# A hybrid decoder trunk with expert retrieval: token rows held in PSUM for the expert dot products, and one pair of banks for the sums

## The chip, the cores and the metric

The kernel runs on one core of a Trainium2 chip. The metric is the device time of one execution in microseconds (us). The time before is 3547.99 us, the median of 3 runs (3546.83 to 3550.83).

## What is computed

Two layers over 512 tokens of width 1024, all in float32. Each layer first mixes three branches (causal pooling, a diagonal state space, dilated attention) through gates and an output projection. Then each token retrieves 128 experts (8 heads of 16) out of 16384. The second half is what the change touches:

```python
def eval_chunk(args):            # chunks of 128 tokens
    hx, e, g = args
    a = jnp.einsum('cd,ckd->ck', hx, u_tab[e])
    return jnp.einsum('ck,ckd->cd', g * jax.nn.gelu(a), v_tab[e])
```

`hx` are the normalized rows of 128 tokens, `e` their 128 expert numbers each, `u_tab` and `v_tab` two tables of 16384 rows of 1024 floats.

## The kernel before, in words

**Tiles and picks.** A tile is 128 tokens, one per partition. Four tiles in each of two layers make 8 tiles (`TILES`). A pick is one expert of every token of a tile, and a tile has 128 picks (`PICKS`), so there are 1024 picks in all. For each pick GpSimd (POOL) issues two gathers by an indirect DMA (line 906). One fetches 128 rows of the first table into one of 6 buffers `rows_u`, the other 128 rows of the second table into one of 6 buffers `rows_v`. Each brings 128 x 4 KB = 512 KB. POOL waits before a gather until its buffer is free: for `rows_u` until VectorE (DVE) has done the dot product six picks back, for `rows_v` until the sum six picks back is done.

**Dots.** For each pick DVE multiplies the 128 rows of `rows_u` with the 128 token rows in `h_tok` and adds up each product (`dot`, line 2105, one custom instruction of 128x1024, the product written over the row). Both inputs lie in SBUF; `h_tok` and `rows_u` are pieces of one tensor `heap`, so the trace shows the dot as heap<-heap. Groups of 8 picks then pass through the GELU on ScalarE (ACT, line 1450) and `weigh` (line 2116), which gives each pick its weight per token.

**Sums.** Twelve picks later the row of `rows_v`, times its weight, is added to the tile's sum. For most picks TensorE (PE) does it (`sum_pick`, line 1166): ACT makes a diagonal matrix of the weights (line 1430), and two matmuls 128x512 accumulate into a pair of PSUM banks. For some odd picks DVE does it (line 1803), into `tile_sum` in SBUF. Tiles take turns on two pairs of banks, 4 and 5 for even tiles, 6 and 7 for odd ones.

**Drain.** At a tile's end (`drain`) DVE joins the PSUM sum and `tile_sum` (lines 2082 and 2084), PE turns the result into columns (8 transposes, line 960), and DVE adds it to `xT` (line 2091). Because the next tile sums into the other pair, its first sum waits only for the drain of the tile two back.

**The token rows.** `h_tok` has two slots, by the tile's parity. PE transposes the normalized columns, and ACT copies them from PSUM to `h_tok` (line 1376, `htok`), after all dots of the tile that had the slot before.

**The order of work.** `make_plan` writes the program as a list of slots. Each slot has at most one dot (`u`) and one sum (`v`), and then a budget of other work for PE, ACT and DVE: the projections, attention, top-16 searches and so on of the next stage, which is computed while the experts of the earlier tiles are retrieved. Every engine runs its instructions in the order of the slots; `GATHERS` lists POOL's gathers in that order too. A stage is 256 tokens, so there are 4. Banks 0 to 3 of PSUM are the ring for all this other work; in the first stage, before the first sums, all 8 banks are. The weights come by other DMAs, issued from the SP queue, into 6 buffers `ring`.

## Time and profile before

| | before |
|---|---|
| median of 3 runs | 3547.99 us |
| profiled execution, its own time | 3563.16 us |
| span of the profiled execution | 3561.4 us |
| PE busy | 3145.3 us (88%) |
| DVE busy | 2528.4 us (71%) |
| POOL busy | 2364.8 us (66%) |
| ACT busy | 962.3 us (27%) |
| moved by DMA | 1305.56 MB, mean 367 GB/s |

The span is from the first to the last instruction of one profiled execution, and its own time is a little longer. Busy time counts the instructions alone. On POOL the issue of a gather counts, which is the time in which it makes the descriptors of the DMA, not the transfer itself. The profiled execution took 15 us more than the median.

### The profile page before, as it was taken

The page shows a single profiled execution, that of the slowest core. Times are in us where ns is not written, and L with a number is a line of the kernel's source. Part 1 is how long each engine was busy: PE and PEld are TensorE (multiplying, and loading weights), DVE is VectorE, ACT ScalarE, POOL GpSimd, SP SyncE. Part 2 cuts the span into 40 slices and gives each one's busy share as a digit, 9 for nine tenths or more (in the row PEclk, how much of TensorE's full clock was granted, in tenths as well). Part 3 has the DMA queues.
Part 4 walks back from the last instruction along what each step waited for, and adds up shares of the span by engine and source line. Part 5 has one row for each costly group of instructions (what it writes and reads, how often), then busy time and mean ns, then how long its engine had stood idle before and what let it go on. Part 6 is the DMA issues. An engine that isn't in the chain of part 4 may idle for free.

```text
span 3561.4 us, 37721 instructions
## 1 busy us (share of the span) xinstructions
PE 3145.3 (88%) x11468; PEld 2012.2 (57%) x11468; DVE 2528.4 (71%) x6159; ACT 962.3 (27%) x2092; POOL 2364.8 (66%) x2114
## 2 busy tenths in 40 slices
PE   8989999979997999968998999979997996667775
PEld 7778756646675656645675656645675652222222
DVE  6556598887656888877656898877666899545444
ACT  2332233343221233332221334333211232111111
POOL 1010276777767776677767777777767777777775
PEclk9989999989999999989999999989999999999998
DMA  5345699999999999999999999999999999999997
GB/s 174 107 175 178 235 407 400 383 397 395 385 409 409 405 392 403 388 400 407 396 409 409 409 405 396 382 397 394 392 409 409 406 390 373 368 373 397 407 408 286
DMA packets 363512, 1305.56 MB, mean 367 GB/s; under 512 B 40432, under 2 KB 44912, under 8 KB 363184
## 3 DMA queue, kind: packets, MB, share of 16 engines
q0 software_dynamic: 298960, 1087.79, 78.1%
q1 hardware_dynamic: 64352, 215.35, 15.9%
q8 instruction: 95, 1.56, 0.2%
q14 instruction: 105, 0.86, 0.1%
HBM read 1288.30 MB, written 14.68 MB: 366 GB/s over the span
## 4 chain that ended last, share of the span: by engine, by line
POOL 36%; PE 31%; issue 13%; DMA 12%; DVE 8%; ACT 0%; DVEq 0%; SPq 0%; POOLq 0%; ACTq 0%
POOL heap L906 36%; PE ps L948 14%; DMA heap<-table_v,heap 11%; PE ps L1166 11%; DVE heap L2105 2%; PE ps L1008 2%; DVE heap L1803 1%; PE ps L1103 1%; PE ps L1047 1%; PE ps L1087 0%; DMA ring<-ssm_par 0%; PE ps L1149 0%; PE ps L1053 0%; PE ps L1019 0%; PE ps L1065 0%
## 5 line engine op out<-in xcount | busy, mean ns | idle before, releaser
L1166 PE MATMUL ps<-heap 128*128 128x512 f32 x3224 | 1599.1, 623 | 345.1 <-DMA heap<-table_v,heap 285.2
L906 POOL DMA_INDIRECT heap<-table_u,heap x1024 | 1162.6, 1135 | 436.2 <-issue 293.7
L2105 DVE CUSTOM_DVE_ANT_0 heap<-heap 128x1024 f32<-128x1024 f32 x1024 | 1243.4, 1220 | 294.0 <-DMA heap<-table_u,heap 286.2
L906 POOL DMA_INDIRECT heap<-table_v,heap x1024 | 1167.6, 1140 | 410.6 <-issue 271.2
L1166 PEld LDWEIGHTS ps<-heap 128*128 128x128 f32 x3224 | 597.7, 196 | 1047.7 <-issue 782.7
L948 PE MATMUL ps<-hT,ring 128*128 128x256 f32 x3840 | 894.6, 383 | 11.2 <-DVE hT L1922 6.2
L948 PEld LDWEIGHTS ps<-hT,ring 128*128 128x128 f32 x3840 | 734.9, 192 | 224.7 <-issue 131.5
L1803 DVE SCALAR_TENSOR_TENSOR heap<-heap 128x1024 f32<-128x1024 f32 x211 | 271.0, 1284 | 362.9 <-issue 242.6
L1430 ACT ACTIVATE heap<-ident,heap 128x128 f32<-128x128 f32 x806 | 297.4, 394 | 543.2 <-PE ps L1166 310.8
L1450 ACT ACTIVATE heap<-heap 128x8 f32<-128x8 f32 x128 | 26.7, 208 | 497.0 <-DVE heap L2105 496.4
L1103 PE MATMUL ps<-temp,ring 128*128 128x256 f32 x640 | 150.6, 383 | 1.5 <-ACT temp L1316 1.0
L1103 PEld LDWEIGHTS ps<-temp,ring 128*128 128x128 f32 x640 | 121.9, 192 | 29.5 <-issue 13.9
L877 POOL DMA_DIRECT2D ssm_par<-heap x8 | 4.5, 566 | 185.4 <-DVEq L1665 185.4
L1335 ACT ACTIVATE temp<-ps 128x512 f32<-128x512 f32 x48 | 28.7, 597 | 350.9 <-PE ps L948 350.8
L948 PE MATMUL ps<-temp,ring 128*128 128x256 f32 x512 | 116.2, 385 | 0.0
L1450 ACT ACT_TABLE_LOAD x89 | 114.2, 1283 | 3.0
L948 PEld LDWEIGHTS ps<-temp,ring 128*128 128x128 f32 x512 | 99.1, 194 | 23.6 <-issue 10.6
L1269 ACT ACTIVATE temp<-ps 32x512 f32<-32x512 f32 x96 | 56.5, 588 | 160.0 <-PE ps L948 159.2
L1008 PE MATMUL ps<-ring,hT 128*128 128x256 f32 x384 | 89.3, 380 | 0.0
L1008 PEld LDWEIGHTS ps<-ring,hT 128*128 128x128 f32 x384 | 72.8, 190 | 25.4 <-issue 17.2
L2105 DVE DVE_READ_ACCUMULATOR2_ANT heap<- 128x1 f32 x1024 | 84.0, 82 | 0.0
L1349 ACT COPY temp<-ps 128x512 f32<-128x512 f32 x32 | 18.7, 586 | 220.9 <-PE ps L948 220.9
(256 smaller groups left out, 2615.2 us busy)
## 6 DMA issues: line engine op xcount, KB each, us to landing
ring<-weights SPq DMA_DIRECT2D x344, 512.0 KB, 7.4
ring<-ssm_par SPq DMA_DIRECT2D x48, 512.0 KB, 7.4
heap<-table_u,heap POOLq DMA_INDIRECT x1024, 9.0
heap<-table_v,heap POOLq DMA_INDIRECT x1024, 8.9
ssm_par<-heap POOLq DMA_DIRECT2D x20, 512.0 KB, 6.6
ring<-weights SPq DMA_DIRECT2D x20, 256.0 KB, 6.1
xT<-x_cm SPq DMA_DIRECT2D x2, 1024.0 KB, 9.3
ssm_par<-heap POOLq DMA_DIRECT2D x8, 256.0 KB, 4.0
```

Source lines behind the costliest of these rows:

```text
L906: pool.indirect_dma_start(rows[:, j, :], None, table, bass.IndirectOffsetOnAxis(expert[:, tile % 2, k:k + 1], 0)).then_inc(landed, 16)
L948: mm = pe.matmul(ps[:, b, i * width:(i + 1) * width], piece(u, name, k * P, P), src[:, k, :], start=(k == 0), stop=(k == rows_n - 1))
L1008: mm = pe.matmul(ps[:, b, tt * 256:(tt + 1) * 256], hT[:, k, tt * P:(tt + 1) * P], piece(u, names[k // 4], (k % 4) * 256, 256), start=(k = ...
L1047: end(pe.matmul(ps[:, b, 0:width], query, kT[part_, m, first:first + width], start=True, stop=True))
L1103: mm = pe.matmul(ps[:, b, j * N:(j + 1) * N], piece(u, ("branch", mm2, br), (rows_n * j + k) * P, P), src[:, k, :], start=(k == 0), stop=( ...
L1166: mm = pe.matmul(ps[:, 4 + 2 * (tile % 2) + half, :], diag[:, PE_TURN[v] % DIAGS, :], rows_v[:, v % NV, half * 512:(half + 1) * 512], star ...
L1269: ins = act.activation(turn_s[to, :], ps[at:at + 32, b, :], ACT.Copy, scale=1.0 if q % 2 else -1.0)
L1335: act.activation(sig[u][:, n % 2, :], ps[:, b, :], ACT.Sigmoid).then_inc(gate_sig, 1)
L1430: act.activation(diag[:, n % DIAGS, :], ident[:], ACT.Copy, scale=w_st[:, g % 3, v % GROUP:v % GROUP + 1]).then_inc(diag_ready, 1)
L1450: act.activation(gelu_st[:, n % 3, :], act_st[:, n % 3, :], ACT.Gelu_apprx_tanh).then_inc(gelued, 1)
L1803: dve.scalar_tensor_tensor(tile_sum, rows_v[:, v % NV, :], w, tile_sum, ALU.mult, ALU.add).then_inc(v_free[v % NV], 1)
L2105: dve.tensor_tensor_reduce(row, row, h_tok[:, tile % 2, :], 1.0, 0.0, ALU.mult, ALU.add, act_st[:, g % 3, pick % GROUP:pick % GROUP + 1]). ...
```

## The change

ACT gets a new piece of work, `hload`, once per tile: after the last dot of the tile before, it copies the tile's token rows from `h_tok` into PSUM banks 6 and 7 (two copies of 128x512). The dots take their second input from there. The sums of all tiles use the one pair 4 and 5, so that the first sum of a tile waits until the drain of the tile before is over (`x_home`). The plan keeps the dots back from a tile's first pick until `hload` is done, the sums until the drain is over, and dots at most 12 picks ahead of sums (`u - v <= LAG`).

```diff
-        htok = (("htok", u // PICKS // 2, u // PICKS % 2, 1), 1)
-        if u < TILES * PICKS and ready([chosen, htok], s):
+        if u < TILES * PICKS and ready([chosen, (("hload", u // PICKS), 0)], s) and u - v <= LAG:
             slot["u"] = u
-        if v < u and v // GROUP * GROUP + GROUP <= u and (v // GROUP * GROUP + GROUP - 1) in end_of \
+        if v < u and (v % PICKS or v == 0 or ready([(("drain", v // PICKS - 1), 2)], s)) and v // GROUP * GROUP + GROUP <= u and (v // GROUP * GROUP + GROUP - 1) in end_of \
...
+        htok = (("htok", tokens // 2, tokens % 2, 1), 1)
+        if tokens < TILES and u == tokens * PICKS and ready([htok], s) and (u == 0 or end_of[u - 1] < s):
+            queue["ACT"].appendleft([("hload", tokens), 0, 1, s])
+            tokens += 1
...
+SUM_BANK, TOKEN_BANK = 4, 6
...
-                        mm = pe.transpose(ps[:, 4 + 2 * (tile % 2) + c // 4, (c % 4) * P:(c % 4 + 1) * P],
+                        mm = pe.transpose(ps[:, SUM_BANK + c // 4, (c % 4) * P:(c % 4 + 1) * P],
...
-                if k == 0 and tile >= 2:
-                    pe.wait_ge(x_home, 2 * (tile - 1))
+                if k == 0 and tile:
+                    pe.wait_ge(x_home, 2 * tile)
...
-                    mm = pe.matmul(ps[:, 4 + 2 * (tile % 2) + half, :], diag[:, PE_TURN[v] % DIAGS, :],
+                    mm = pe.matmul(ps[:, SUM_BANK + half, :], diag[:, PE_TURN[v] % DIAGS, :],
...
-                        act.wait_ge(dotted, PICKS * (2 * u - 1 + t))
+                        act.wait_ge(h_there, 2 * (2 * u - 1 + t))
...
+                elif kind == "hload":
+                    tile = item[1]
+                    act.wait_ge(h_copied, 2 * (tile + 1))
+                    if tile:
+                        act.wait_ge(dotted, PICKS * tile)
+                    else:
+                        for b in range(TOKEN_BANK, TOKEN_BANK + 2):
+                            act.wait_ge(bank_free[b], BANK_TOTAL[b])
+                    for half in range(2):
+                        act.copy(ps[:, TOKEN_BANK + half, :], h_tok[:, tile % 2, 512 * half:512 * half + 512]).then_inc(h_there, 1)
+                        yield
...
                 if pick % PICKS == 0:
-                    dve.wait_ge(h_copied, 2 * (tile + 1))
+                    dve.wait_ge(h_there, 2 * (tile + 1))
...
-                dve.tensor_tensor_reduce(row, row, h_tok[:, tile % 2, :], 1.0, 0.0, ALU.mult, ALU.add,
+                token = ps[:, TOKEN_BANK:TOKEN_BANK + 2, :].rearrange("p i c -> p (i c)")
+                dve.tensor_tensor_reduce(row, row, token, 1.0, 0.0, ALU.mult, ALU.add,
```

The plan has 1249 slots before and 1270 in the changed kernel; the number of sums on DVE goes from 218 to 221. Where a tile ends, the order moves. On PE, around the end of the second tile, before (L1166 are the sums, L948 and L1116 projections and key scores of the next stage, L960 the transposes of the drain):

```order
L1166 MATMUL ps<-heap 128x512 x2
L948 MATMUL ps<-hT,ring 128x256 x4
L1166 MATMUL ps<-heap 128x512 x2
L960 MATMUL ps<-ident,heap 128x128 x8
L1166 MATMUL ps<-heap 128x512 x2
L948 MATMUL ps<-hT,ring 128x256 x3
L1166 MATMUL ps<-heap 128x512 x4
```

and in the changed kernel, whose line numbers are higher (L1173 the sums, L955 and L1123 the other work, L967 the transposes):

```order
L955 MATMUL ps<-hT,ring 128x256 x3
L1173 MATMUL ps<-heap 128x512 x4
L1123 MATMUL ps<-keysT,temp 128x128 x4
L955 MATMUL ps<-hT,ring 128x256 x9
L967 MATMUL ps<-ident,heap 128x128 x8
L955 MATMUL ps<-hT,ring 128x256 x7
L1173 MATMUL ps<-heap 128x512 x4
```

Before, sums of the next tile stand ahead of the transposes; now all sums of the next tile stand behind them, and 16 projection matmuls stand between the last sum of one tile and the first of the next. On DVE at the same place, before (L2105 are the two instructions of a dot, L2082 and L2091 the two ends of the drain, the rest is the search for the 16 best):

```order
L2105 ISA heap<-heap 128x1024
L2105 ISA heap 128x1
L2082 TENSOR_TENSOR heap<-heap,ps 128x512 x2
L1845 MAX_INDEX heap<-heap 128x8
L2105 ISA heap<-heap 128x1024
L2105 ISA heap 128x1
L1850 MAX heap<-heap 128x8 x2
L1854 MAX_INDEX heap<-heap 128x8 x2
L1856 TENSOR_TENSOR heap<-heap 128x256
L2105 ISA heap<-heap 128x1024
L2105 ISA heap 128x1
L2091 TENSOR_TENSOR xT<-xT,ps 128x4x128 x2
```

and changed (L2123 the dot, L2099 and L2108 the drain):

```order
L2123 ISA heap<-heap,ps 128x1024
L2123 ISA heap 128x1
L2099 TENSOR_TENSOR heap<-heap,ps 128x512 x2
L1922 TENSOR_SCALAR heap<-heap 128x16
L1924 SCALAR_TENSOR_TENSOR heap<-heap 128x16
L2123 ISA heap<-heap,ps 128x1024
L2123 ISA heap 128x1
L1930 TENSOR_SCALAR heap<-heap 128x16
L1856 MAX heap<-heap 128x8 x2
L1860 MATCH_REPLACE heap<-heap 128x128 x2
L2108 TENSOR_TENSOR xT<-xT,ps 128x4x128 x2
```

One dot instead of two stands between the two ends of the drain, and the dots read `ps` beside `heap`. On ACT the new copies stand between its usual work (L1448 the diagonals, L1369 and L1371 copies of key scores, L1468 the GELU):

```order
L1468 ACT_TABLE_LOAD
L1468 ACTIVATE heap<-heap 128x8
L1448 ACTIVATE heap<-ident,heap 128x128
L1396 COPY ps<-heap 128x512 x2
L1369 COPY heap<-ps 128x256
L1371 COPY heap<-ps 128x256
L1448 ACTIVATE heap<-ident,heap 128x128
```

Whatever stands behind the two copies on ACT, a diagonal for the sums among it, waits with them for the last dot of the tile.

## Rows read from the trace of the kernel before

**Rows 1.** The page: span, busy time of each engine, DMA rate in 40 slices.

```profile
span 3561.4 us, 37721 instructions
PE 3145.3 (88%) x11468; PEld 2012.2 (57%) x11468; DVE 2528.4 (71%) x6159; ACT 962.3 (27%) x2092; POOL 2364.8 (66%) x2114
GB/s 174 107 175 178 235 407 400 383 397 395 385 409 409 405 392 403 388 400 407 396 409 409 409 405 396 382 397 394 392 409 409 406 390 373 368 373 397 407 408 286
```

**Rows 2.** One line's instructions: gathers, duration min/median/max, idle before them, time to landing.

```profile
L906 POOL DMA_INDIRECT heap<-table_u,heap x1024: 935/942/2025, 412.0 to 3515.4; - x171
L906 POOL DMA_INDIRECT heap<-table_v,heap x1024: 935/941/2819, 435.5 to 3537.1; - x171
...
  issue: 564.9, 1830
...
DMA to landing us min/median/max: 4.4/8.9/19.6
```

**Rows 3.** Costliest groups of the page: busy, mean ns of one, idle before.

```profile
L906 POOL DMA_INDIRECT heap<-table_u,heap x1024 | 1162.6, 1135 | 436.2 <-issue 293.7
L2105 DVE CUSTOM_DVE_ANT_0 heap<-heap 128x1024 f32<-128x1024 f32 x1024 | 1243.4, 1220 | 294.0 <-DMA heap<-table_u,heap 286.2
L906 POOL DMA_INDIRECT heap<-table_v,heap x1024 | 1167.6, 1140 | 410.6 <-issue 271.2
L1803 DVE SCALAR_TENSOR_TENSOR heap<-heap 128x1024 f32<-128x1024 f32 x211 | 271.0, 1284 | 362.9 <-issue 242.6
```

**Rows 4.** Stretches: length; PE, PEld, DVE, ACT, POOL busy (count); PE clock; DMA share; GB/s.

```profile
600.00:700.00 100.00, 100.00 (x350) 61.70 (x349) 85.54 (x250) 32.76 (x71) 70.26 (x62) 1.00 1.00 383
1400.00:1500.00 100.00, 100.00 (x362) 65.05 (x361) 82.39 (x249) 34.12 (x73) 65.88 (x61) 1.00 1.01 387
1800.00:1900.00 100.00, 95.60 (x376) 71.32 (x375) 60.17 (x91) 18.78 (x32) 67.38 (x58) 0.98 1.03 409
2200.00:2300.00 100.00, 100.00 (x354) 62.69 (x353) 84.39 (x254) 34.51 (x71) 70.22 (x62) 1.00 1.00 385
2300.00:2400.00 100.00, 80.32 (x317) 47.91 (x315) 82.00 (x174) 35.73 (x79) 79.78 (x67) 0.85 1.00 390
3000.00:3100.00 100.00, 67.11 (x138) 23.03 (x136) 69.88 (x189) 20.85 (x54) 78.96 (x70) 1.00 0.97 362
3400.00:3500.00 100.00, 74.18 (x151) 25.35 (x149) 49.74 (x86) 14.02 (x39) 76.45 (x78) 0.99 1.03 408
```

**Rows 5.** The same view for two long stretches: with other work, and the tail.

```profile
400.00:2900.00 2500.00, 2311.26 (x8554) 1521.17 (x8554) 1912.81 (x4574) 726.96 (x1553) 1833.14 (x1585) 0.96 1.01 398
2900.00:3523.00 623.00, 451.87 (x964) 163.67 (x962) 373.95 (x848) 117.68 (x304) 484.68 (x455) 0.99 1.00 386
```

**Rows 6.** Timeline (start, duration): gathers that begin while a dot runs.

```profile
1508.50 1.20 DVE L2105 CUSTOM_DVE_ANT_0 heap<-heap 128x1024 f32<-128x1024 f32 x1
1509.09 1.42 POOL L906 DMA_INDIRECT heap<-table_v,heap  x1 [0.30 <-issue]
...
1511.50 1.22 DVE L2105 CUSTOM_DVE_ANT_0 heap<-heap 128x1024 f32<-128x1024 f32 x1
1512.24 1.29 POOL L906 DMA_INDIRECT heap<-table_v,heap  x1 [0.30 <-issue]
```

**Rows 7.** Timeline: gathers beside DVE instructions with one input in PSUM.

```profile
1259.71 1.29 DVE L2091 TENSOR_TENSOR xT<-xT,ps 128x512 f32<-128x512 f32 x2 [2.10 <-PE ps L960]
1260.02 0.94 POOL L906 DMA_INDIRECT heap<-table_u,heap  x1 [0.30 <-issue]
...
2405.38 0.69 DVE L1974 CUSTOM_DVE_ANT_0 temp<-ps,mask 128x512 f32<-128x512 f32 x1
2405.73 0.94 POOL L906 DMA_INDIRECT heap<-table_u,heap  x1 [0.60 <-DVE heap L2105]
```

**Rows 8.** DVE by shape: the same custom instruction with its first input in PSUM.

```profile
L1974 DVE CUSTOM_DVE_ANT_0 temp<-ps,mask 128x512 f32<-128x512 f32 x16 | 11.0, 689 | 2.3 <-PE ps L1047 1.6 <-DVE stats L1974 0.7
L1974 DVE CUSTOM_DVE_ANT_0 temp<-ps,mask 128x256 f32<-128x256 f32 x16 | 6.8, 423 | 2.0 <-DVE stats L1974 2.0
```

**Rows 9.** ACT: a pass of 128x512 from SBUF (min/median/max).

```profile
L1197 ACT ACTIVATE hT<-xT x16: 612/613/630, 6.5 to 2100.2; 128x512 f32<-128x512 f32 x16
```

**Rows 10.** Timeline of the second tile's drain: last sums, join, transposes.

```profile
1250.03 1.88 PE L1166 MATMUL ps<-heap 128*128 128x512 f32 x4
...
1251.95 1.28 DVE L2082 TENSOR_TENSOR heap<-heap,ps 128x512 f32<-128x512 f32 x2 [1.21 <-PE ps L1166]
...
1258.63 1.04 PE L960 MATMUL ps<-ident,heap 128*128 128x128 f32 x8
```

More of the change, by code:

```diff
@@ L172 @@
     "ptab": ("DVE",), "tb": ("PE", "ACT"), "wt": ("PE", "ACT", "DVE"), "drain": ("DVE", "PE", "DVE"),
-    "final": ("ACT", "PE", "ACT", "DVE"),
+    "final": ("ACT", "PE", "ACT", "DVE"), "hload": ("ACT",),
 }
@@ L191, in weight_of @@
     if eng == "ACT":
-        return {"squares": (4, .6), "final": (4 if part == 0 else 1, .6), "mean": (1, .5), "ssm_u": (16, .29), "ssm_y": (16, .29), "q": (4, .6), "k": (4, .6),
+        return {"squares": (4, .6), "hload": (2, .6), "final": (4 if part == 0 else 1, .6), "mean": (1, .5), "ssm_u": (16, .29), "ssm_y": (16, .29), "q": (4, .6), "k": (4, .6),
                 "att_e": (1, .25 + .0011 * att_blocks(item[2]) * P) if kind == "att_e" else 0, "att_o": (1, .3), "mix": (2, .4),
@@ L405, in make_plan @@
     shut = []
+    tokens = 0
     finals = deque(range(len(FINALS)))
@@ L738, in trunk @@
         h_copied = sem("h_copied")
+        h_there = sem("h_there")
         shifted = sem("shifted")
@@ L1159, in sum_pick @@
                 pe.wait_ge(v_landed[v % NV], 16 * (v // NV + 1))
-                if k == 0 and tile >= 2:
-                    pe.wait_ge(x_home, 2 * (tile - 1))
+                if k == 0 and tile:
+                    pe.wait_ge(x_home, 2 * tile)
                 elif k == 0:
-                    for b in range(4 + 2 * tile, 6 + 2 * tile):
+                    for b in range(SUM_BANK, SUM_BANK + 2):
                         pe.wait_ge(bank_free[b], BANK_TOTAL[b])
                 for half in range(2):
-                    mm = pe.matmul(ps[:, 4 + 2 * (tile % 2) + half, :], diag[:, PE_TURN[v] % DIAGS, :],
+                    mm = pe.matmul(ps[:, SUM_BANK + half, :], diag[:, PE_TURN[v] % DIAGS, :],
                                    rows_v[:, v % NV, half * 512:(half + 1) * 512], start=(k == 0), stop=(k == PICKS - 1))
@@ L2070, in emit @@
                     tile = item[1]
-                    at = 4 + 2 * (tile % 2)
                     if part == 0:
@@ L2081, in emit @@
                             if mine:
-                                dve.tensor_tensor(to, to, ps[:, at + half, :], ALU.add).then_inc(sum_joined, 1)
+                                dve.tensor_tensor(to, to, ps[:, SUM_BANK + half, :], ALU.add).then_inc(sum_joined, 1)
                             else:
-                                dve.tensor_copy(to, ps[:, at + half, :]).then_inc(sum_joined, 1)
+                                dve.tensor_copy(to, ps[:, SUM_BANK + half, :]).then_inc(sum_joined, 1)
                             yield
@@ L2090, in emit @@
                             dst = xT[:, 4 * half:4 * half + 4, t0:t0 + P]
-                            dve.tensor_tensor(dst, dst, ps[:, at + half, :].rearrange("p (k c) -> p k c", k=4),
+                            dve.tensor_tensor(dst, dst, ps[:, SUM_BANK + half, :].rearrange("p (k c) -> p k c", k=4),
                                               ALU.add).then_inc(x_home, 1)
```

## The prediction

> **What bounds the kernel now.** I read the page first, then the stretches, then single instructions. The page [rows 1] names PE as the busiest engine, at 88%, but its DMA row is more telling: from the sixth slice to the last but one the rate stays between 368 and 409 GB/s and stands at exactly 409 again and again. That is a ceiling. 409 GB/s means 524,288 B / 409 GB/s = 1.28 us per gather, with nothing else moving.
>
> What keeps the rate under the ceiling is to be read in the stretches [rows 4]. To use them one needs a fact about POOL. A gather occupies it for 0.94 us at least, and in 1830 cases the profile shows an idle piece of 564.9 / 1830 = 0.31 us before it in which POOL waited for nothing ("issue") [rows 2]. So POOL's occupied time is busy time plus about 0.30 us per gather:
> - 3000 to 3100: 78.96 + 70 x 0.30 = 100 us. POOL is full, the DMAs move 362 GB/s, PE is at 67%.
> - 2300 to 2400: 79.78 + 67 x 0.30 = 99.9 us, 390 GB/s, PE at 80%. Full again.
> - 1800 to 1900: 67.38 + 58 x 0.30 = 85 us at 409 GB/s. Here the DMAs bound.
> - 600 to 700, 1400 to 1500, 2200 to 2300: POOL occupied for 84 to 89 us, 383 to 387 GB/s, PE at 100 us of 100. Here PE bounds.
> - 3400 to 3500: POOL is full and the rate is 408: both at once.
>
> All three limits lie close together, and they take turns. The two long stretches [rows 5] give the sum. In the tail (2900 to 3523) POOL is occupied for 484.7 + 455 x 0.30 = 621 of 623 us at 386 GB/s; against 409 that loses 623 x 23 / 409 = 35 us. In 400 to 2900 it is occupied for 2309 of 2500 us at 398 GB/s; the loss is 2500 x 11 / 409 = 67 us, of which the first 12 us precede the first gather (it starts at 412.0 [rows 2]).
>
> **Why POOL is slow.** Most gathers take the minimum: the medians are 941 and 942 ns, but the means 1135 and 1140 [rows 2, 3]. The excess is 1162.6 + 1167.6 - 2048 x 0.94 = 405 us of POOL time. The timeline shows where it arises [rows 6]. A dot runs from 1508.50 to 1509.70; a gather that begins at 1509.09 takes 1.42 us, and ends 0.81 us after the dot's end. The next pair: dot until 1512.72, gather from 1512.24 for 1.29 us, end again 0.81 us after the dot's. The gather, then, waits for the dot's end. Beside DVE instructions with one input in PSUM it does not [rows 7]: one that begins 0.31 us into L2091 (its inputs SBUF, then PSUM, as in the new dot) and one that begins 0.35 us into L1974 (the dot's own custom instruction, PSUM first) both take 0.94 us.
>
> **The change, part by part.**
>
> 1. *The dots' second input moves to PSUM.* By rows 7 they should no longer hold up gathers. What is the dots' share of the 405 us? The other instructions as long, with both inputs in SBUF, are the sums on DVE, 271 us busy against 1243 [rows 3]; with shorter ones I give 75% to the dots, 300 us. Gathers then take on average 0.94 + 105 / 2048 = 0.99 us, with 0.30 us of issue 1.29; in the tail, where hardly any sums are on DVE, about 1.25, just under the 1.28 us of the ceiling. POOL stops being a limit of its own.
>  - Tail: of the 35 us lost I keep 5 for the drain and the end. Gain 28 to 30, taken as 28.
>  - 400 to 2900: 67 - 12 = 55 us to be had. The stretches in which PE is full lose about 26 + 22 + 24 GB/s each over 100 us, 18 us together, and more at their edges; I count 20 as PE's. Of the other 35 I take two thirds, 23 us, since PE is busy for 2311 of 2500 us there and will be reached more often once gathers come sooner. Bounds: 0 and 55.
> 2. *The price of the dot itself.* The trace has no dot with an input in PSUM, but the same custom instruction with its first input there [rows 8]: 423 ns for 256 columns, 689 for 512, so 1.04 ns per column and 157 ns fixed, and 157 + 1024 x 1.04 = 1.22 us for 1024. That is today's 1220 ns [rows 3]. I count nothing. The Trainium skill (VectorE: DVE Perf Modes, the section on the TRN2 errata) has a table that speaks against the change: a fixed 58 cycles for SBUF sources, 120 for PSUM. At 0.96 GHz that would be an estimated 65 ns more per dot, 66 us of DVE time over 1024 dots. The rows above speak against it; even by it, DVE at 71% could hide most.
> 3. *`hload`.* Two ACT passes of 128x512 from SBUF take 0.61 us each [rows 9]; to PSUM unseen, taken the same. With semaphores the first dot of a tile comes some 1.5 us after the last one of the tile before; for seven boundaries that is 10 us of DVE delay if nothing covered it. On ACT 8 x 1.2 = 10 us are added to 962; behind the copies wait a diagonal and, through it, one sum. Cover: `rows_u` has six buffers, gathers land 8.9 us after issue [rows 2], so while the dots pause POOL goes on and DMAs in flight go on. Counted as 0.
> 4. *One pair of banks.* PE's last sum of a tile, DVE's join (1.28 us), the transposes (1.04 us) and DVE's add (1.29 us) now form a chain ahead of the next tile's first sum. Bare it takes 3.6 us; with what stands between on each engine it is, in today's trace, from 1251.9 (the last sum done) to 1261.0, 9.1 us [rows 10, 7]. PE has 16 projections to do meanwhile and loses perhaps 2 us; where there is no other work (last tiles) it has time anyway. The sum buffers cover the DMAs: six gathers to `rows_v` with as many to `rows_u` are 12 x 1.28 = 15 us of transfers, more than the chain. I count 0.7 us per boundary where PE is near full, 5 us in all. Bounds: 0 if covered, 7 x (9.1 + 1.5) = 74 us if not at all.
> 5. *Extra slots.* 21 more slots hold no dot or sum, but also no gather; they move other work to a tile's end, which would be done anyway. 0, as part of item 4. The order POOL issues in hardly shifts. SP's queue is untouched.
>
> Sum: -28 - 23 + 5 = -46 us, on the profiled 3563.2 gives 3517. The median stands 15.2 us lower, so 3502 us.
>
> **Rivals.**
> - *PE takes over at once* in 400 to 2900: a mechanism seen in rows 4 at three places. Then only the tail gains: 3548 - 28 + 5 = 3525. PE's 92% speaks for it, its many waits for landings against it. 0.18.
> - *The full yield*: nearly all that is lost against the ceiling comes back, 30 + 50, for boundaries that cost nothing: 3468. 0.12.
> - *The boundaries are not covered* (the other side). The drain chain and `hload` stall sums and dots, buffers fill, POOL stops, and the DMAs run dry. It decides from the point where a stall outlasts the buffers, about 15 us less the 5 us or so that a gather takes to land (the least seen is 4.4 [rows 2]): some 10 us against a chain of 9.1. Close, where other waits add to it. At the full 74 us against a gain of 51: 3571; at half, 3534. For over 3555: 0.10.
> - *The change doesn't free POOL.* The Trainium skill (SBUF — State Buffer, Who interferes with whom) infers that tensor_tensor instructions do not hold up descriptor generation, which needs the write interface. The 0.81 us behind each dot's end contradict this for gathers, as does the same section's rule that two SBUF inputs contend with a GpSimd instruction that reads SBUF. If the stretch had another cause, item 1 were 0 and the time 3548 + 5 = 3553. 0.06.
>
> **How the numbers follow.** My forecast, 3502 with about 15 either way, has 0.54. The range reaches to the full yield and past the rival of 3525: 3468 to 3546. What a measurement of this kernel can tell from no change is about 0.2%, 7 us. Faster by more: 0.54 + 0.18 + 0.12, less a little where boundaries eat the gain, 0.82. Slower by more: 0.10. Between: 0.08.
>
> **What would show it.** Right: mean gather near 1.00 us; no gather stretched by a dot; POOL occupied for clearly less than 100 us per 100 in the tail, at over 400 GB/s there; dots of 1.22 us; less POOL idle time from "issue" and more from waits for dots and sums. Wrong: dots at 1.28 us (item 2); at the seven tile ends stretches of 20 us with the rate well under 400 (item 4); PE at 100% in more stretches while the rate stays at 385 (first rival). The prediction fails if gathers stay near 1.14 us, or if a tile end costs more than 5 us.

## The result, and the profile after

| | before | changed |
|---|---|---|
| median, timed side by side (5 runs each) | 3549.54 us | 3530.55 us |
| ratio of the changed kernel to the one before | | 0.9939 (95%: 0.9919 to 0.9958) |
| span of the profiled execution | 3561.4 us | 3528.7 us |
| POOL busy | 2364.8 us | 2065.4 us |
| mean of a gather, two tables | 1135 and 1140 ns | 989 and 993 ns |
| mean of a dot | 1220 ns | 1214 ns |

The profiled execution of the kernel before took 3563.16 us, 13.6 us more than the median; that of the changed kernel is the median itself. So the spans differ by more than the times do.

The kernel is faster by 0.61%, 22 us of 3550 (15 to 29). The forecast was 46 us. The direction and POOL's relief came as forecast, the amount was just under half.

The page of the changed kernel, its head, its chain by engine and its costliest groups (busy us, mean ns of one, idle before and what ended it), as in [rows 1] and [rows 3]:

```profile
span 3528.7 us, 37718 instructions
PE 3132.2 (89%) x11456; PEld 2007.1 (57%) x11456; DVE 2528.2 (72%) x6162; ACT 969.2 (27%) x2106; POOL 2065.4 (59%) x2114
GB/s 176 108 177 186 226 409 398 390 400 409 407 409 409 409 374 397 397 404 403 409 409 409 409 386 378 382 407 407 406 409 409 407 355 373 409 409 410 409 409 307
PE 49%; DMA 22%; DVE 15%; POOL 7%; issue 5%; ACT 1%; DVEq 0%; SPq 0%; ACTq 0%; POOLq 0%
L2123 DVE CUSTOM_DVE_ANT_0 heap<-heap,ps 128x1024 f32<-128x1024 f32 x1024 | 1237.6, 1214 | 301.4 <-DMA heap<-table_u,heap 294.0
L913 POOL DMA_INDIRECT heap<-table_v,heap x1024 | 1017.1, 993 | 630.5 <-PE ps L1173 411.2
L913 POOL DMA_INDIRECT heap<-table_u,heap x1024 | 1012.8, 989 | 486.6 <-issue 234.5
```

POOL has 300 us less work, and its gathers of the second table now wait 411 us for PE's sums (L1173). All of POOL's waits for that line were 138.3 us before. POOL is no longer what holds things up: it had 36% of the chain that ended last, now 7%. The DMA rate has more slices at 409, and three dips where it had 392, 396 and 390 before: 374, 378 and 355.

A dot no longer delays a gather. Counted over the whole trace, 892 gathers of the kernel before begin while a dot runs; they take 1277 ns in the mean, 301 us more in sum than 0.94 us each. In the changed kernel there are 752 such gathers, with a mean of 942 ns and 1.5 us in sum above 0.94 each. In the example from the timeline the second row begins 0.34 us after the first, whose dot runs on to 1259.88, and takes the minimum (compare [rows 6]):

```profile
1258.67 1.21 DVE L2123 CUSTOM_DVE_ANT_0 heap<-heap,ps 128x1024 f32<-128x1024 f32 x1
1259.01 0.94 POOL L913 DMA_INDIRECT heap<-table_v,heap  x1 [0.30 <-issue]
```

By stretches (columns as in [rows 4]), first the two long ones, then a piece of the tail, one in which PE is full, 25 us at the ends of the second, fourth and sixth tile, and the 100 us at the beginning of the tail:

```profile
400.00:2900.00 2500.00, 2306.08 (x8581) 1520.00 (x8579) 1943.08 (x4699) 745.39 (x1591) 1593.15 (x1587) 0.97 1.01 398
2900.00:3490.00 590.00, 441.07 (x908) 158.59 (x908) 340.70 (x722) 105.06 (x279) 427.58 (x452) 0.97 1.02 404
...
3000.00:3100.00 100.00, 75.89 (x157) 26.49 (x156) 47.81 (x84) 15.21 (x42) 75.36 (x81) 1.00 1.03 409
600.00:700.00 100.00, 100.00 (x345) 60.94 (x345) 86.28 (x255) 29.64 (x66) 61.39 (x63) 1.00 1.00 387
1250.00:1275.00 25.00, 25.00 (x93) 15.52 (x92) 24.26 (x78) 8.87 (x21) 16.49 (x17) 1.00 0.87 302
2050.00:2075.00 25.00, 20.19 (x57) 10.90 (x58) 24.11 (x64) 8.70 (x19) 13.52 (x15) 0.86 0.91 337
2850.00:2875.00 25.00, 19.19 (x51) 10.35 (x50) 22.85 (x64) 7.43 (x16) 12.74 (x14) 0.80 0.85 312
...
2900.00:2950.00 50.00, 36.67 (x73) 14.77 (x74) 48.29 (x161) 12.16 (x30) 34.13 (x35) 0.90 0.99 383
2950.00:3000.00 50.00, 36.30 (x71) 14.25 (x70) 45.14 (x131) 14.28 (x33) 34.79 (x37) 0.90 0.99 372
```

In the tail 3000 to 3100 went from 362 to 409 GB/s, over the 400 of the forecast. How much of that is the operand's doing is taken up below. The 100 us before it stay at 383 and 372; they had 384 and 373 in the kernel before. DVE is busy there for 48.3 and 45.1 of 50 us, and POOL no longer full. From 400 to 2900 the rate is 398, what it was [rows 5]. The stretches that POOL had slowed are at the ceiling now or near it (2300 to 2400 has 406), but the ends of three tiles have fallen to 302, 337 and 312; in the kernel before all three stretches have 409.

What happens there differs from end to end. First the timeline of the second tile's end (compare [rows 10]):

```profile
1236.41 3.60 PE L1173 MATMUL ps<-heap 128*128 128x512 f32 x8
...
1240.73 4.05 PE L955 MATMUL ps<-hT,ring 128*128 128x256 f32 x18
...
1244.62 1.04 PE L967 MATMUL ps<-ident,heap 128*128 128x128 f32 x8
1245.49 3.19 PE L955 MATMUL ps<-hT,ring 128*128 128x256 f32 x14
1245.69 1.28 DVE L2108 TENSOR_TENSOR xT<-xT,ps 128x512 f32<-128x512 f32 x2 [1.88 <-PE ps L967]
...
1248.52 3.60 PE L1173 MATMUL ps<-heap 128*128 128x512 f32 x8
...
1250.67 0.94 POOL L913 DMA_INDIRECT heap<-table_v,heap  x1 [6.78 <-PE ps L1173]
...
1253.28 1.88 PE L1173 MATMUL ps<-heap 128*128 128x512 f32 x4
...
1256.72 1.88 PE L1173 MATMUL ps<-heap 128*128 128x512 f32 x4
```

The last sums end at 1240.0, the next tile's first begin at 1248.5. PE is not idle for a moment of these 8.5 us; it does the other work of the slots that have no sum. POOL meanwhile finds no free buffer for 6.78 us. After that PE gives a sum every 3.44 us (1253.28 to 1256.72), no faster than the kernel before at the same place (1253.47 to 1256.92), so it doesn't make up for the pause:

```profile
1253.47 1.88 PE L1166 MATMUL ps<-heap 128*128 128x512 f32 x4
...
1256.92 1.88 PE L1166 MATMUL ps<-heap 128*128 128x512 f32 x4
```

At the ends of the fourth and the sixth tile it is otherwise. There PE stands still and waits for DVE's add, 3.56 and 2.72 us, after it has waited for DVE's join (2.54 and 3.09 us, not shown). POOL stops for 5.86 and 5.99 us:

```profile
2055.90 5.33 PE L1173 MATMUL ps<-heap 128*128 128x512 f32 x8 [3.56 <-DVE xT L2108]
...
2059.79 0.94 POOL L913 DMA_INDIRECT heap<-table_v,heap  x1 [5.86 <-PE ps L1173]
...
2845.98 5.41 PE L1173 MATMUL ps<-heap 128*128 128x512 f32 x12
...
2859.13 8.20 PE L1173 MATMUL ps<-heap 128*128 128x512 f32 x12 [2.72 <-DVE xT L2108]
...
2863.16 0.94 POOL L913 DMA_INDIRECT heap<-table_v,heap  x1 [5.99 <-PE ps L1173]
```

The two rows of 12 are the same work, 5.41 us ahead of the drain and 8.20 behind it. The granted clock of 2850 to 2875 is 0.80 in the mean, where the kernel before has 1.00. So the first sums behind such a standstill are slower too.

A tile's end, then, is a gap in the sums, of 8.5, about 7.2 and 7.7 us at these three. It is filled by listed work at the first of them and by the drain's chain at the two others.

### The profile page after: what moved, and what is told of

Its sections match the earlier page's. It is cut to its first block, busy times and chain, and to the rows that moved or that the text cites. A ratio compares the mean times of both kernels' runs of the same rounds, so it can differ in the third digit from the quotient of the medians.

```text
span 3528.7 us, 37718 instructions
## 1 busy us (share of the span) xinstructions
PE 3132.2 (89%) x11456; PEld 2007.1 (57%) x11456; DVE 2528.2 (72%) x6162; ACT 969.2 (27%) x2106; POOL 2065.4 (59%) x2114
## 4 chain that ended last, share of the span: by engine, by line
PE 49%; DMA 22%; DVE 15%; POOL 7%; issue 5%; ACT 1%; DVEq 0%; SPq 0%; ACTq 0%; POOLq 0%
PE ps L1173 19%; PE ps L955 19%; DMA heap<-table_v,heap 18%; POOL heap L913 7%; DVE heap L2123 6%; DMA heap<-table_u,heap 3%; PE ps L1110 3%; PE ps L1015 2%; PE ps L1094 2%; DVE heap L1821 1%; PE ps L1072 1%; PE ps L1054 1%; PE ps L1060 1%; PE ps L1123 0%; DVE temp L1723 0%
## 5 line engine op out<-in xcount | busy, mean ns | idle before, releaser
L1173 PE MATMUL ps<-heap 128*128 128x512 f32 x3212 | 1589.3, 623 | 309.2 <-DMA heap<-table_v,heap 193.7
L2123 DVE CUSTOM_DVE_ANT_0 heap<-heap,ps 128x1024 f32<-128x1024 f32 x1024 | 1237.6, 1214 | 301.4 <-DMA heap<-table_u,heap 294.0
L913 POOL DMA_INDIRECT heap<-table_v,heap x1024 | 1017.1, 993 | 630.5 <-PE ps L1173 411.2
L913 POOL DMA_INDIRECT heap<-table_u,heap x1024 | 1012.8, 989 | 486.6 <-issue 234.5
L1173 PEld LDWEIGHTS ps<-heap 128*128 128x128 f32 x3212 | 598.6, 196 | 1013.7 <-issue 723.6
L955 PE MATMUL ps<-hT,ring 128*128 128x256 f32 x3840 | 891.9, 382 | 11.0 <-DVE hT L1940 6.0
L955 PEld LDWEIGHTS ps<-hT,ring 128*128 128x128 f32 x3840 | 731.6, 192 | 221.1 <-issue 127.1
L1448 ACT ACTIVATE heap<-ident,heap 128x128 f32<-128x128 f32 x803 | 295.2, 393 | 506.1 <-PE ps L1173 299.1
L1468 ACT ACTIVATE heap<-heap 128x8 f32<-128x8 f32 x128 | 26.7, 209 | 474.2 <-DVE heap L2123 473.5
L955 PE MATMUL ps<-temp,ring 128*128 128x256 f32 x512 | 114.8, 382 | 0.0
L955 PEld LDWEIGHTS ps<-temp,ring 128*128 128x128 f32 x512 | 98.2, 192 | 22.6 <-issue 9.9
L2123 DVE DVE_READ_ACCUMULATOR2_ANT heap<- 128x1 f32 x1024 | 84.2, 82 | 0.0
```

Of the source, the lines that this page charges most:

```text
L913: pool.indirect_dma_start(rows[:, j, :], None, table, bass.IndirectOffsetOnAxis(expert[:, tile % 2, k:k + 1], 0)).then_inc(landed, 16)
L955: mm = pe.matmul(ps[:, b, i * width:(i + 1) * width], piece(u, name, k * P, P), src[:, k, :], start=(k == 0), stop=(k == rows_n - 1))
L1173: mm = pe.matmul(ps[:, SUM_BANK + half, :], diag[:, PE_TURN[v] % DIAGS, :], rows_v[:, v % NV, half * 512:(half + 1) * 512], start=(k == 0) ...
L1448: act.activation(diag[:, n % DIAGS, :], ident[:], ACT.Copy, scale=w_st[:, g % 3, v % GROUP:v % GROUP + 1]).then_inc(diag_ready, 1)
L1468: act.activation(gelu_st[:, n % 3, :], act_st[:, n % 3, :], ACT.Gelu_apprx_tanh).then_inc(gelued, 1)
L2123: dve.tensor_tensor_reduce(row, row, token, 1.0, 0.0, ALU.mult, ALU.add, act_st[:, g % 3, pick % GROUP:pick % GROUP + 1]).then_inc(dotted, 1)
```

## The experiments

All times are medians; ratios are to the kernel before, timed in the same session, with 95% intervals. Where I give a difference in us, it is the ratio's difference times 3550; between two runs it carries some 10 us either way, so a single one of 8 or 14 us is barely clear of nothing. Rows of one run come from one execution.

**One bank per tile.** The sum's two halves go to one bank, tiles alternate between banks 4 and 5, and the plan's condition for the drain is left out. The list then has 1 slot without a sum at a tile's end, where the changed kernel has 3.

```diff
-                if k == 0 and tile:
-                    pe.wait_ge(x_home, 2 * tile)
+                if k == 0 and tile >= 2:
+                    pe.wait_ge(x_home, 2 * (tile - 1))
...
-                    mm = pe.matmul(ps[:, SUM_BANK + half, :], diag[:, PE_TURN[v] % DIAGS, :],
+                    mm = pe.matmul(ps[:, SUM_BANK + tile % 2, :], diag[:, PE_TURN[v] % DIAGS, :],
```

> The changed kernel without the wait of a tile's first sum for the drain of the tile before: the two halves of a pick's sum go into one bank, and tiles take banks 4 and 5 in turn (so the two halves are added up into one: this part of the output is left out). Dots still read PSUM, hload stays, PE does the same matmuls. Theory A (the drain chain at the ends of the second, fourth and sixth tile empties the DMA queue, some 8 + 5 + 12 us): 3530 - 25 = about 3505 us, and no stretch of 25 us under 380 GB/s at those tile ends. Theory B (PE's own work sets the time from 400 to 2900, and what is lost at a tile's end would be lost elsewhere): 3525 to 3531 us.

Measured: 3514.87 us, ratio 0.9901 (0.9878 to 0.9924). That is 14 us better than the changed kernel (3 to 24), where theory A wanted 25 and theory B none. The same three stretches of time:

```profile
1250.00:1275.00 25.00, 25.00 (x90) 16.11 (x89) 24.13 (x77) 6.67 (x15) 15.83 (x17) 1.00 0.99 373
2050.00:2075.00 25.00, 23.09 (x71) 11.75 (x71) 24.34 (x70) 13.19 (x25) 16.04 (x17) 1.00 1.02 403
2850.00:2875.00 25.00, 20.65 (x57) 10.35 (x56) 24.30 (x72) 12.37 (x27) 17.14 (x19) 1.00 0.97 364
```

373, 403 and 364 GB/s in place of 302, 337 and 312: (71 + 66 + 52) x 25 / 409 = 12 us of transfers, which is most of the 14. (The tile ends come 4 to 12 us earlier in this run; summed over 50 us around each of the seven ends, the DMAs lack 10 us of transfers to 409 GB/s here and 23 in the changed kernel, a difference of 13.) The expectation that none would be under 380 failed for two; in these DVE is busy for 24 of 25 us.

**Only the pair of banks.** The kernel before with the sums on banks 4 and 5 and the plan's two conditions, without `hload`, dots from SBUF.

```diff
-                if k == 0 and tile >= 2:
-                    pe.wait_ge(x_home, 2 * (tile - 1))
+                if k == 0 and tile:
+                    pe.wait_ge(x_home, 2 * tile)
```

> The kernel before with only the sums moved to one pair of banks, and the plan's two conditions for it; dots read SBUF, no hload. Theory A: the chain costs what it costs in the changed kernel, 15 to 25 us, so 3549 + 20 = about 3569 us. Theory B: no more than 5 us, 3549 to 3554 us.

Measured: 3566.73 us, ratio 1.0042 (1.0023 to 1.0061), 15 us slower than before (8 to 22). The single pair and its list cost as much without the new dots as with them (14 us).

**Only `hload`.** The one-bank kernel with dots that read `h_tok` again.

```diff
-                dve.tensor_tensor_reduce(row, row, token, 1.0, 0.0, ALU.mult, ALU.add,
+                dve.tensor_tensor_reduce(row, row, h_tok[:, tile % 2, :], 1.0, 0.0, ALU.mult, ALU.add,
```

> As the first of these runs (one bank per tile, no drain wait, the two halves of the sum added into one bank), but the dots read SBUF again while they still wait for ACT's copies. Against the kernel before it has only hload's wait and copies. Covered, as predicted: 3549 to 3553 us. If hload's pause costs some 2 us at each of seven tile ends: 3563 us. Against the first run it gives the price of dots that read SBUF with all else equal: 30 to 50 us if POOL's delay is worth what the prediction said.

Measured: 3553.29 us, ratio 1.0004 (0.9985 to 1.0023). That is 1 us more, between 5 less and 8 more: ACT's copies and the dots' wait for them cost nothing that can be measured. The step from here to the one-bank kernel is the second input of the dots and no more: 0.9901 against 1.0004, 37 us. From the pair-only run to the changed kernel it is the same step: 0.9939 against 1.0042, 37 us again. So the dots' operand is worth 37 us (26 to 47) and the tile ends cost 14 or 15, whichever way they are combined. The gathers of this run:

```profile
L913 POOL DMA_INDIRECT heap<-table_u,heap x1024 | 1158.1, 1131 | 441.5 <-issue 294.2 <-DVE heap L2121 92.6 <-DVE heap L1929 54.8
L913 POOL DMA_INDIRECT heap<-table_v,heap x1024 | 1156.1, 1129 | 414.5 <-issue 272.6 <-PE ps L1172 139.8 <-DVE heap L2121 2.1
```

Their means are 1131 and 1129 ns, as before the change, with `hload` in place; it is the operand that frees POOL.

Where the 37 us arise is seen from the starts of the first, the 1537th and the last of the 2048 gathers, the 1537th standing about where the last two tiles begin (us from the span's start):

| run | first | 1537th | last | first to 1537th | 1537th to last |
|---|---|---|---|---|---|
| before | 412.0 | 2829.9 | 3537.1 | 2417.9 | 707.2 |
| changed | 409.5 | 2823.1 | 3503.4 | 2413.6 | 680.3 |
| one bank per tile | 407.4 | 2807.2 | 3486.2 | 2399.8 | 679.0 |
| only the pair | 412.4 | 2850.7 | 3542.1 | 2438.3 | 691.4 |
| only `hload` | 406.4 | 2832.8 | 3523.0 | 2426.4 | 690.2 |
| only the plan's conditions (below) | 410.1 | 2842.8 | 3537.0 | 2432.7 | 694.2 |

The step to dots from PSUM gives 27 us up to the 1537th gather and 11 after it with one bank per tile (last but one row against the third), and 25 and 11 with the pair (fourth against second). So only 11 us of it lie in the last two tiles. Each number is of one execution, but the two pairs agree. The profiled execution of the kernel before took 707 us for these two, but the three others with dots from SBUF took 690 to 694. Whether their lists or a slow stretch in that one execution make this difference is open.

**A shorter chain.** Less other work in the slots of a drain.

```diff
+        draining = v and v % PICKS == 0 and v < TILES * PICKS and not ready([(("drain", v // PICKS - 1), 2)], s)
+        if draining:
+            pe, dve = min(pe, 1.3), min(dve, 1.2)
...
-        for name in ("TOP", "DVE", "SPIN", "PREP") if due else ("DVE", "SPIN", "TOP", "PREP"):
+        for name in ("TOP", "DVE", "SPIN", "PREP") if due and not draining else ("DVE", "SPIN", "TOP", "PREP"):
```

> The changed kernel, complete, with a shorter chain: while a drain is under way the plan gives PE at most 1.3 us and DVE at most 1.2 us of other work per slot and DVE does the drain first, so 4 instead of 8 projection matmuls stand ahead of the transposes and 4 instead of 7 behind them. Theory A: about 4 of 8.5 us fewer at the second tile's end, 8 to 12 us in all, 3520 us. Theory B: unchanged, 3528 to 3533 us.

Measured: 3527.2 us, ratio 0.9917 (0.9895 to 0.9939). That is 8 us better than the changed kernel by the ratios, in the direction of theory A, but the intervals overlap, so it isn't shown.

**Less work for PE, dots from PSUM.** The one-bank kernel with `for half in range(1)` in `sum_pick`, which leaves out half of the output's columns.

> The run with one bank per tile (dots read PSUM, no drain wait), and with the second of the two matmuls of each sum on PE left out: half of that part of the output is missing, PE has 0.94 us less per pick and some 760 us less in all; DMAs, dots and plan are the same. Theory B2 (what the one-bank run, 3515 us, still lacks to the DMAs' ceiling is PE's doing): the 1241 MB from the first gather on at 409 GB/s take 3034 us, so 410 + 3034 + 40 = about 3484 us, at 405 GB/s or more from 400 to 2900. Rival (DVE's order, landings and the plan hold it back): 3505 to 3515 us.

**Less work for PE, dots from SBUF.** The same edit on the `hload` run.

> The same relief for PE (second matmul of each sum left out), but the dots read SBUF: the run with hload alone, 3553 us, less PE work. If POOL with its delayed gathers is a bound of its own, as the prediction read it: only the stretches come back in which PE was full, 15 to 20 us, so about 3535 us, and the distance to the run before, with dots in PSUM, grows from 38 to 50 us or more. If PE was the bound nearly everywhere: both near 3484 us.

Measured: 3502.58 us, ratio 0.9865 (0.9846 to 0.9884), and 3518.71 us, ratio 0.9923 (0.9903 to 0.9942). With dots in PSUM PE's relief brings 13 us, with dots in SBUF 29. The distance between the two operands is 21 us (11 to 30) in place of 37 (26 to 47); I had expected it to grow to 50, and that is refuted. That it shrinks is likely, at the edge of what these runs can tell. Their long stretches:

```profile
400.00:2900.00 2500.00, 2010.35 (x7454) 1368.22 (x7452) 1952.23 (x4729) 751.93 (x1607) 1593.84 (x1608) 0.88 1.02 403
```

(dots from PSUM) and

```profile
400.00:2900.00 2500.00, 2014.60 (x7423) 1364.30 (x7421) 1949.70 (x4701) 749.26 (x1603) 1880.09 (x1606) 0.88 1.02 402
```

(dots from SBUF). With PE at 80%, a POOL that is occupied for 1880 + 1606 x 0.30 = 2362 of 2500 us still reaches 402 GB/s. So POOL at over 90% was not a bound by itself there. The reading that fits is that it was one together with a PE at 92%, each preventing that the other catch up; how they do it wasn't followed. Theory B2 is not borne out in full: 13 of the 31 us that the one-bank kernel lacks to 3484 were PE's. Of the remaining 18 us, some 10 lie in 2900 to 3000, where this run has 367 and 371 GB/s with DVE busy for 48.3 and 41.3 of 50 us: (42 + 38) x 50 / 409. What bounds there is DVE by these rows, not by a run with less work for it. The granted clock of the whole run fell to 0.844 with PE's load (0.960 in the one-bank run); PE's busy time fell from 3145 to 2774 us, 371 us, and not by the 760 of the expectation.

**A bank for the transposes.** The ring gets 3 banks, bank 3 takes the transposes in two parts, and the next tile's sums wait only for the join.

```diff
-                if k == 0 and tile:
-                    pe.wait_ge(x_home, 2 * tile)
+                if k == 0 and tile:
+                    pe.wait_ge(sum_joined, 2 * tile)
...
-BANK = [n % (8 if n < EARLY else 4) for n in range(len(RING_UNITS))]
+BANK = [n % (8 if n < EARLY else 3) for n in range(len(RING_UNITS))]
```

> The changed kernel, complete, with the chain cut: the ring gets 3 banks, and bank 3 is kept for the drain's transposes, 4 at a time, so the next tile's first sum waits only for DVE's join (1.3 us) instead of join, transposes and add. Theory A: the tile ends cost no more than in the one-bank run, 3515 us, plus what a ring of 3 costs (next run). If the ring costs nothing: 3515. Rival: the smaller ring makes PE wait for copies and the plan holds dots back more often (its list has 43 slots with a dot missing, not 26), 3540 us or more.

**Its control: a ring of 3 banks in the kernel before.** The second part of that diff alone.

> The kernel before with a ring of 3 banks instead of 4 for the other work and nothing else: the price of the smaller ring by itself. If PE finds its banks free anyway: 3549 to 3553 us. If each unit now waits for the copy of the unit three back: 3560 us or more.

Measured: 3555.66 us, ratio 1.0018 (1.0008 to 1.0028), and 3615.32 us, ratio 1.0170 (1.0144 to 1.0196). The fourth bank of the ring is worth 60 us, more than anything the change touches. Part of this may be the list: with 3 banks it has 1280 slots instead of 1249, 8 to 12 slots without a sum at the second, fourth and sixth tile's end, and 248 sums on DVE instead of 218. On a ring of 3 the new dots with the cut chain gain 54 us, but as a version this loses. Theory A's sum, 3515 + 60 = 3575, came out 19 us too high. The run can't tell what cutting the chain brings, since its list has gaps of 6, 6 and 12 slots at three ends.

**A seventh buffer for the second table**, in the room of one slot of `h_tok`, and **the same with the shorter chain**.

```diff
-NV = 6
+NV = 7
...
-        h_tok = hcut(2 * D).rearrange("p (i d) -> p i d", i=2)
+        h_tok = hcut(D)
...
-                        act.wait_ge(h_there, 2 * (2 * u - 1 + t))
+                        act.wait_ge(h_there, 2 * (2 * u + t))
```

> The changed kernel, complete, with a seventh buffer for the rows of the second table. The room comes from the token rows: since the dots read PSUM, one slot of h_tok is enough (ACT fills it when hload of the tile before is over). Theory A (a tile's end costs what its chain is longer than the buffers last): each of the three costly ends is 2.6 us shorter for the DMAs (a pair of gathers more ahead), and PE's full stretches are bridged a little better: 3530 - 10 = 3520 us. Rival (the dots' six buffers stop POOL at the same point): 3528 to 3532 us.

> The same with the shorter chain (3527 us by itself). Theory A: both shorten the same gap, 3527 - 10 = 3517 us, near the one-bank run's 3515, which is as far as a better tile end can bring it. Rival: 3525 to 3530 us.

Measured: 3527.52 us, ratio 0.9942 (0.9924 to 0.9960), and 3521.46 us, ratio 0.9925 (0.9902 to 0.9949). The buffer brings nothing that can be told in either (0.9939 and 0.9917 without it); theory A had 10 us for it, and the rival's range holds for the first.

**Only the plan's two conditions.** The kernel before with two pairs of banks, its waits unchanged; sums and dots merely stand later in the list.

```diff
-        if u < TILES * PICKS and ready([chosen, htok], s):
+        if u < TILES * PICKS and ready([chosen, htok], s) and u - v <= LAG:
...
-        if v < u and v // GROUP * GROUP + GROUP <= u and (v // GROUP * GROUP + GROUP - 1) in end_of \
+        if v < u and (v % PICKS or v == 0 or ready([(("drain", v // PICKS - 1), 2)], s)) and v // GROUP * GROUP + GROUP <= u and (v // GROUP * GROUP + GROUP - 1) in end_of \
```

> The kernel before with only the plan's two conditions (sums of a tile wait in the list for the drain of the one before, dots at most 12 ahead), still with two pairs of banks, so PE waits for no drain. It parts the 15 us that one pair cost without PSUM dots. Theory A1 (the wait itself costs): 3550 to 3555 us. Rival A2 (the list costs: 3 to 4 slots per tile without gathers' consumers, in which PE and DVE do other work): near the 3566 us of the one-pair run.

Measured: 3568.01 us, ratio 1.0050 (1.0034 to 1.0065). With no wait for the drain of the tile before, the list alone costs 18 us (12 to 23), as much as the single pair (15). The ends of its second, fifth and sixth tile:

```profile
1255.00:1280.00 25.00, 25.00 (x98) 16.91 (x97) 22.27 (x77) 7.82 (x19) 14.21 (x14) 1.00 0.89 323
2475.00:2500.00 25.00, 25.00 (x118) 18.80 (x117) 16.46 (x26) 8.25 (x14) 18.96 (x18) 0.99 0.87 321
2880.00:2905.00 25.00, 20.74 (x57) 10.11 (x55) 24.29 (x71) 7.65 (x16) 17.77 (x16) 1.00 0.89 311
```

323, 321 and 311 GB/s, with PE busy for all 25 us at two of them: the dips are there without the wait. Rival A2 holds in this kernel, with dots from SBUF: the list alone makes a gap that costs as much as list and wait together. It has 1271 slots in place of 1249, and 3 of them, once 4, without a sum at each tile's end where there were none. The list of the `hload` run has 1 such slot at each end and the same limit of 12 picks, and costs nothing measurable, so it is the condition for the drain that costs. For the changed kernel this doesn't rule out the wait, since there PE does stand still at two ends.

**The gap in the list, shortened.** The first sum may stand right behind the transposes; then also less other work per slot and seven buffers; then also dots that go on.

```diff
-        if v < u and (v % PICKS or v == 0 or ready([(("drain", v // PICKS - 1), 2)], s)) and v // GROUP * GROUP + GROUP <= u and (v // GROUP * GROUP + GROUP - 1) in end_of \
+        if v < u and (v % PICKS or v == 0 or ready([(("drain", v // PICKS - 1), 1)], s)) and v // GROUP * GROUP + GROUP <= u and (v // GROUP * GROUP + GROUP - 1) in end_of \
```

> The changed kernel, complete, with one word of the plan changed: a tile's first sum may stand in the list as soon as the transposes stand ahead of it, not only after DVE's add; PE still waits for the add by its semaphore. The gap of a tile's end is 2 slots without a sum instead of 3, the real chain is the same. Theory L (what costs is the other work that the list puts into the gap on PE and DVE, not the chain): a third of the 16 us that lie between the changed kernel and the one-bank run comes back, 3524 us or less. Rival W (the wait for the drain costs): 3528 to 3532 us, since the wait is no shorter.

> The same, with at most 1.3 us of PE's and 1.2 us of DVE's other work per slot while the transposes are outstanding, and the seventh buffer. Theory L: PE has only the chain itself between the last sum and the next tile's first, 4 to 5 us instead of 8.5 at the second tile's end, which the buffers cover: 3515 to 3519 us, as the one-bank run. Rival W: no better than the 3521 us of the short chain with seven buffers.

> The same as the run before, and without the rule that keeps the dots at most 12 picks ahead of the sums, so the dots go on through the gap. If DVE's missing dots are part of the cost: 2 to 5 us less than the run before. If the sums alone stop POOL (its gathers alternate, so one stopped table stops both): the same within 3 us.

Measured: 3528.36 us, ratio 0.9932 (0.9913 to 0.9951); 3523.6 us, 0.9919 (0.9898 to 0.9941); 3523.41 us, 0.9916 (0.9896 to 0.9935). The first step alone can't be told from the changed kernel: theory L wanted 3524 or less, and the range of rival W holds. The second missed theory L's 3515 to 3519 as well. The second and third come to 0.9919 and 0.9916, 7 to 8 us better, as the shorter chain did alone, and within their intervals. That the dots go on in the third brings nothing that can be told. The second tile's end in the run with all of it but the dots:

```profile
1242.84 1.88 PE L1176 MATMUL ps<-heap 128*128 128x512 f32 x4
...
1244.76 1.28 DVE L2102 TENSOR_TENSOR heap<-heap,ps 128x512 f32<-128x512 f32 x2 [2.66 <-PE ps L1176]
...
1246.10 1.09 PE L970 MATMUL ps<-ident,heap 128*128 128x128 f32 x8
...
1247.79 1.28 DVE L2111 TENSOR_TENSOR xT<-xT,ps 128x512 f32<-128x512 f32 x2
...
1249.21 1.78 PE L1176 MATMUL ps<-heap 128*128 128x512 f32 x2 [2.02 <-DVE xT L2111]
```

From the last sum's end at 1244.7 to the next at 1249.2 it is 4.5 us in place of 8.5. Of these PE now waits for 2.02 us. Over the whole run PE's waits for DVE's add are 7.7 us in three places in the changed kernel and 5.2 in three with the shorter chain alone, but 11.2 in six, 12.1 in seven and 16.0 in six in these three runs, where the first sum stands earlier in the list. What the list puts into a gap and the drain's chain run side by side, and by these rows the longer of the two decides: a first sum that stands earlier waits for the chain.

The four versions with less other work in the gap stand at 0.9916 to 0.9925 and beat the kernel before clearly. Against the changed kernel (0.9939) they all lie on the better side, but no one interval is clear of its. The lowest median of a complete kernel is 3521.46 us, the seventh buffer with the shorter chain, and the lowest ratio 0.9916, the run with the dots going on; the four can't be told apart.

## Why the prediction was right and wrong

**What bounds the kernel: right in what it saw, too simple in how it added.** Ceiling of 409 GB/s, POOL full, PE full in three stretches: all this stands. But the shortfall was charged to one engine at a time, and DVE wasn't among the three limits. In the two runs with less work for PE the operand is worth 21 us, not 37, and a nearly full POOL loses little. And from 2900 to 3000 DVE is busy for 45 to 48 of each 50 us and the rate stays at 372 to 383 in the changed kernel, 8 us that the text gave to POOL.

**Item 1, the dots' operand: mechanism right, its term for the tail too large. This is the larger part of the miss.** Gathers went from 1138 to 991 ns in the mean, 0.99 as forecast, and what the dots had added to gathers was 301 us, as worked out. The yield was put at 28 + 23 = 51 us and measured at 37, twice (26 to 47). By the starts of the gathers, one execution of each run, the 23 us for 400 to 2900 are about right (25 and 27), and it is the 28 us for the tail that failed: 11 in both pairs of runs. The text read a loss of 35 us from the tail of one execution, one that took 13.6 us more than the median, put all of it down to POOL and kept 5; three other runs with dots from SBUF were through the last two tiles 13 to 17 us sooner than that one.

**Item 2, the dot's own price: right.** 1214 ns against the 1220 worked out from the custom instruction with its input in PSUM. The other number weighed there was an estimate of 65 ns more, from the table's 58 cycles for SBUF sources and 120 for PSUM (the Trainium skill, VectorE: DVE Perf Modes, the section on the TRN2 errata). This trace contradicts it for an instruction with one of its two inputs in PSUM: 6 ns less.

**Item 3, `hload` at 0: right.** The run with `hload` alone: +1 us (-5 to +8).

**Items 4 and 5, the tile ends at 5 us: the other step that failed.** The runs show 14 to 15 (one bank against two, pair only), and 18 for the list alone. The text set PE's loss at 2 us per end, called the extra slots free because their other work "would be done anyway", and said that the buffers cover 12 x 1.28 = 15 us. The work is done anyway, and at the second tile's end PE was indeed never idle. But while it is done no row is summed and buffers stay full: POOL stopped 3.9 us after the last sum there, and for 6.78 us. So the buffers didn't hold 15 us of transfers when the gap began; that some held landed rows waiting for their slot would explain it, but wasn't counted. The order rows in the change's section showed 16 projection matmuls between the sums. In the trace each is two rows, 18 + 14 = 32 of them, and they take 4.05 + 3.19 = 7.2 us, not 2; with the scores and transposes the gap could have been read from them. At the fourth and sixth tile's end PE waited for the chain itself, 3.56 and 2.72 us for its last link. How the cost in the changed kernel divides between list and chain stays open: the list alone makes as large a cost with dots from SBUF, a list with less work in the gap took back 7 or 8 us by the ratios, not clear of noise, and where the first sum stood earlier PE waited longer for the add.

**The rivals.** "PE takes over at once" gave 3525 and comes nearest to 3530.55 in number, but for another reason: the operand did yield in 400 to 2900 (25 to 27 us) and less than 28 in the tail (11), and the tile ends took 14 of it back. That the forecast's nearest rival fits the number is luck. "The boundaries are not covered" had the right mechanism, at a fifth of its full price of 74 us. "The change doesn't free POOL" is refuted; the gathers that begin within a dot went from 1277 to 942 ns with its operand. The inference behind the rival (the Trainium skill, SBUF — State Buffer, Who interferes with whom), that tensor_tensor instructions do not hold up descriptor generation, does not carry over to these gathers and this custom instruction with two SBUF inputs.

**Taken together:** forecast -51 + 5 = -46 us, measured -37 + 14 = -23 by the single runs, -22 by the changed kernel itself. Of the 23 us between forecast and measurement 14 are item 1's and 9 those of items 4 and 5.

## What to carry to other kernels

When an engine is moved off a shared bound, count as gain only what the next engine at over 90% lets through: try the relief with that engine's load cut as well. Look for an engine that is full in a stretch before charging that stretch to another, and read a loss from more than one execution. In a kernel that runs from a list of slots, a slot without the consumer of a buffer is a pause for the DMAs even if every engine is busy in it; read its length from the work that the list puts there and compare it with the buffers that are free then, not with all of them. Look at more than one such gap: here other work filled one, and the wait the next.

## What the runs showed of the hardware that I had not expected

- The first input in SBUF and the second in PSUM is enough to keep a 128x1024 custom instruction on DVE from delaying POOL's indirect DMAs: with all but the dots' operand and one of ACT's waits the same the mean of 2048 gathers fell from 1130 to 987 ns (`hload` run against one bank).
- The DMAs hold 409 GB/s for 100 us at a time on one core, in the changed kernel's tail 409 or 410 in five slices of the page in a row. No slice of any run's page is above 410.
- ACT writes 128x512 from SBUF to PSUM in 576 ns at the median (16 copies), beside 613 for its square from SBUF to SBUF [rows 9].
- Half of the sums' matmuls taken away lowered the granted TensorE clock over the run from 0.960 to 0.844, and the matmuls that were left took 786 ns in the mean, not 625. So less work for PE gave back less time than it held.
